# RWKV scan of a fused network on one core: the inverse of each chunk in seven products instead of ten, and the products with k and v on the other diagonal of the array

## The reference, cut to what matters

```
def _wkv_step(S, inp):
    r_t, w_t, k_t, v_t, a_t, b_t = inp
    sa = jnp.einsum('zbhvk,zbhk->zbhv', S, a_t)
    S = S * w_t[..., None, :] + sa[..., :, None] * b_t[..., None, :] + v_t[..., :, None] * k_t[..., None, :]
    return S, jnp.einsum('zbhvk,zbhk->zbhv', S, r_t)
```

## Time and profile before

| | |
|---|---|
| median of 3 runs | 4038.56 us (4037.82 to 4040.61) |
| span of the profiled execution (its own time is given as this span alone) | 4039.7 us |
| TensorE, DVE, ScalarE, GpSimd busy in the span | 3727.0, 2360.8, 1204.0, 1321.7 us |
| scan, first to last mask of a head | 2814.2 to 3365.6 us |
| walk of the last head in `walk_finish` | from some 3398.5 to 3424 us |

### The profile page before, as it was taken

The page is one execution under the profiler, slowest core; times in us unless marked ns, Lnnn a source line. Parts: engine busy times, 40 slices in busy tenths (PEclk is TensorE's granted clock), DMA queues, the critical chain, the costliest instruction groups (busy, mean ns, idle before and its releaser), DMA issues. The chain is left out here.

```text
span 4039.7 us, 81581 instructions
## 1 busy us (share of the span) xinstructions
PE 3727.0 (92%) x32706; PEld 2683.2 (66%) x32706; DVE 2360.8 (58%) x3864; ACT 1204.0 (30%) x2668; POOL 1321.7 (33%) x1020
## 2 busy tenths in 40 slices
PE   8888999898999999899999997998999999899887
PEld 6667878657787898777344444874999998733333
DVE  4568882545985445565444445767888776623333
ACT  3352222344222322331111112224455454111112
POOL 4443444434445364573000000431555453000000
PEclk9999999999999999999999999999999999899999
DMA  4114542303554122345999995356333234589997
GB/s 128 56 53 170 184 157 93 104 1 105 178 187 146 66 96 75 99 138 228 404 420 420 420 420 212 134 177 201 88 89 91 78 93 147 199 366 422 421 421 316
DMA packets 231204, 787.80 MB, mean 195 GB/s; under 512 B 56008, under 2 KB 64024, under 8 KB 171136
## 3 DMA queue, kind: packets, MB, share of 16 engines
q1 hardware_dynamic: 225008, 764.12, 50.9%
q0 software_dynamic: 5328, 19.40, 1.2%
q10 hardware_dynamic: 576, 0.09, 0.0%
HBM read 736.15 MB, written 47.38 MB: 194 GB/s over the span
## 5 line engine op out<-in xcount | busy, mean ns | idle before, releaser
L2887 POOL DMA_INDIRECT moe0e_xg<-moe_h,moe_first_rows x20 | 18.9, 947 | 546.3 <-DVE moe_first_rows L3044 540.5
L3011 ACT ACT_TABLE_LOAD x32 | 41.1, 1283 | 519.2 <-PE moe1e_p_u L2957 262.4
L373 POOL TENSOR_TENSOR gmi_w_lo<-gmi_rows_w,gmi_w_hi 128x512 fp32r<-128x512 f32 x64 | 120.2, 1878 | 159.8 <-ACT gmi_w_hi L415 159.8
L3960 PE MATMUL scan_bank<-scan_T,scan_off 64*64 64x64 f32 x3840 | 159.4, 220 | 8.5 <-issue 5.7
L373 POOL TENSOR_TENSOR p_w_lo<-p_rows_w,p_w_hi 128x512 fp32r<-128x512 f32 (+3 forms) x88 | 113.5, 1291 | 159.9 <-ACT p_w_hi L415 159.9
L2887 POOL DMA_INDIRECT moe1e_xg<-moe_h,moe_first_rows x17 | 16.0, 940 | 451.0 <-DVE moe_first_rows L3044 444.4
L1159 POOL TENSOR_TENSOR f0u_w_lo<-f0u_w,f0u_w_hi 128x1024 fp32r<-128x1024 f32 x42 | 115.0, 2757 | 137.6 <-ACT f0u_w_hi L1175 137.6
L1159 POOL TENSOR_TENSOR f1u_w_lo<-f1u_w,f1u_w_hi 128x1024 fp32r<-128x1024 f32 x42 | 114.3, 2742 | 137.5 <-ACT f1u_w_hi L1175 137.5
L1227 DVE SCALAR_TENSOR_TENSOR f0u_ada<-hT,condition,f0u_ada 128x512 f32<-128x512 f32 x168 | 148.2, 949 | 16.4 <-DMA hT<-in_ada_w_dram 15.9
L1227 DVE SCALAR_TENSOR_TENSOR f1u_ada<-hT,condition,f1u_ada 128x512 f32<-128x512 f32 x168 | 140.5, 903 | 20.5 <-DMA hT<-in_ada_w_dram 20.0
L2984 PE MATMUL moe0e_p_y<-moe_ring,moe0e_gatedT 128*64 128x512 f32 x608 | 137.6, 605 | 7.8 <-ACT moe0e_gatedT L3013 7.8
(11 more groups left out here) (903 smaller groups left out, 11529.7 us busy)
## 6 DMA issues: line engine op xcount, KB each, us to landing
moe_ring<-in_moe_w_down_dram SPq DMA_DIRECT2D x140, 1024.0 KB, 18.0
gm_uT<-in_moe_w_gu_dram SPq DMA_DIRECT2D x111, 1024.0 KB, 16.6
moe_ring<-in_moe_w_gu_dram SPq DMA_DIRECT2D x102, 1024.0 KB, 24.7
walk_memory<-in_moe_w_gu_dram SPq DMA_DIRECT2D x60, 1024.0 KB, 24.4
hT<-in_ada_w_dram SPq DMA_DIRECT2D x48, 1024.0 KB, 6.8
f0u_w<-in_ffn_w_gate_up_dram SPq DMA_DIRECT2D x22, 1024.0 KB, 4.8
f1u_w<-in_ffn_w_gate_up_dram SPq DMA_DIRECT2D x22, 1024.0 KB, 4.8
gmi_rows_w<-in_ga_w_in_dram SPq DMA_DIRECT2D x64, 256.0 KB, 2.7
```

Source lines behind the costliest of these rows:

```text
L373: nc.gpsimd.tensor_tensor(w_lo[t % 2][:, 0:width], w[t % RAW][:, 0:width], w_hi[t % 2][:, 0:width], ALU.subtract).then_inc(w_lo_made, 1)
L2887: pool.indirect_dma_start(xg[:], None, H.h, bass.IndirectOffsetOnAxis(rows[:, 0:1], 0)).then_inc(gathered, 16)
L3011: nc.scalar.activation(sg[:], p_g[:], ACT.Silu).then_inc(silu_ready, 1)
L3960: mm = nc.tensor.matmul(out[r], lhsT[r], rhs[r], start=start, stop=stop, skip_group_check=True)
```

## The change

The inverse is made by powers. A is split in three: joins of size 1 (first join), all joins of sizes 2 to 16 together (off), and the join of size 32 (off_outer). N = T times off is nilpotent; R is multiplied up by 1 + N, 1 + N^2, 1 + N^4 and 1 + N^8 while N is squared. There are seven products for each group of four chunks (n = 0 to 20): FIRST (off times T), three that square and multiply at once with 128 columns ([W | R] streamed through Z), LAST_POWER, OUTER (off_outer times T) and FINAL. The three wide ones are issued in two halves, so that 30 units (`UNITS`) keep the places of walk parts and factor slots. Each power is copied by ScalarE after DVE's addition (same bank) and transposed by DVE.

Direction 0's v now lies on hi and direction 1's on lo, and every product with kh or with v goes by `crossed`: hi rows to lo outputs and lo rows to hi outputs. Bonus rows and masks follow. Products with b and with k go to different banks and are issued in turn. Since a straight and a crossed product may not accumulate in one place at once, TensorE waits for its own products by four new semaphores. `walk_share` issues dS before the rows (in `walk_finish` it was after them), and x and y from v for the next chunk behind it. `walk_finish` has the same new walk (its diff repeats the one of the scan and is left out).

```diff
-LEVELS = 5
+BLOCK_BITS = 5
+PRODUCTS = 7
...
+    NI = PRODUCTS * NG
+    ADDED, COPIED, TURNED = 5 * NG, 5 * NG, 6 * NG
+    FIRST, LAST_POWER, OUTER, FINAL = 0, 4, 5, 6
+    UNITS = [(n, part) for n in range(NI) for part in ((0, 4),) * (n // NG not in (1, 2, 3)) + ((0, 2), (2, 4)) * (n // NG in (1, 2, 3))]
+    TURNS_BEFORE = (2, 3, 2, 3)
+    INV_BANK = (2, 1, 3, 0)
...
+    BPAIR_BANK, KPAIR_BANK = (4, 0, 2), (1, 3, 4)
+    TURN_BANKS = (slice(0, 2), slice(2, 4), slice(0, 2))
+    SLOTS = len(UNITS) // 2
...
-            for z, rows in ((0, lo), (1, hi)):
+            for z, rows in ((0, hi), (1, lo)):
...
+            if h:
+                pool.wait_ge(s["r_added"], h * ADDED)
             for g in range(NG):
+                g4 = slice(4 * g, 4 * g + 4)
                 pool.wait_ge(s["scaled"], h * NG + g + 1)
-                if h >= 2:
-                    pool.wait_ge(s["sa_ready"], (h - 1) * STEPS)
-                nc.gpsimd.tensor_tensor(R[u][:, 4 * g:4 * g + 4, :], strict(u, g), over4(join[:, 0, :]), ALU.mult).then_inc(s["r_joined"], 1)
-            for n in range(NZ):
-                l, g = n // NG, n % NG
-                if h:
-                    pool.wait_ge(s["z_ready"], (h - 1) * NZ + n + 1)
-                nc.gpsimd.tensor_tensor(off[n][:], strict(u, g), over4(join[:, l + 1, :]), ALU.mult).then_inc(s["off_ready"], 1)
+                nc.gpsimd.tensor_tensor(WR[:, g4, 1, :], strict(u, g), over4(join[:, 0, :]), ALU.mult).then_inc(s["r_joined"], 1)
+                nc.gpsimd.tensor_tensor(off[:, g4, :], strict(u, g), over4(join[:, 1, :]), ALU.mult).then_inc(s["off_ready"], 1)
+            for g in range(NG):
+                nc.gpsimd.tensor_tensor(off_outer[:, 4 * g:4 * g + 4, :], strict(u, g), over4(join[:, 2, :]), ALU.mult).then_inc(s["outer_ready"], 1)
...
             def copy_z(n):
-                act.wait_ge(s["z_ready"], h * NZ + n + 1)
-                if n >= 2:
-                    act.wait_ge(s["zr_ready"], h * NZ + n - 1)
-                A(Z[n % 2][:], quad(z_bank[n % 2]), ACT.Copy).then_inc(s["z_copied"], 1)
-            copy_z(0)
-            walk_part(walk, -1)
-            for n in range(NZ):
-                if n + 1 < NZ:
-                    copy_z(n + 1)
-                walk_part(walk, 2 * n)
-                walk_part(walk, 2 * n + 1)
-                if ahead is not None:
-                    factor_part(ahead, n)
+                act.wait_ge(s["inv_ready"], h * NI + n + 1)
+                A(Z[:, chunks(n), :], one(n), ACT.Copy).then_inc(s["z_copied"], 1)
+            def copy_power(n):
+                act.wait_ge(s["r_added"], h * ADDED + adds_through(n))
+                A(WR[:, chunks(n), 0, :], both(n)[:, :, 0, :], ACT.Copy).then_inc(s["z_copied"], 1)
+            for k, (n, (first, end)) in enumerate(UNITS):
+                if n // NG in (FIRST, OUTER):
+                    copy_z(n)
+                walk_part(walk, k - 1)
+                if squares(n) and end == 4:
+                    copy_power(n)
+                if ahead is not None and k % 2 == 0 and k:
+                    factor_part(ahead, k // 2 - 1)
+            walk_part(walk, len(UNITS) - 1)
...
+            def add_product(n):
+                g4 = chunks(n)
+                if n // NG == FIRST or n // NG == OUTER:
+                    return
+                dve.wait_ge(s["inv_ready"], h * NI + n + 1)
+                if squares(n):
+                    V.tensor_tensor(WR[:, g4, 1, :], WR[:, g4, 1, :], both(n)[:, :, 1, :], ALU.add).then_inc(s["r_added"], 1)
+                elif n // NG == LAST_POWER:
+                    V.tensor_tensor(WR[:, g4, 1, :], WR[:, g4, 1, :], one(n), ALU.add).then_inc(s["r_added"], 1)
+                else:
+                    if h >= 2 and n % NG == 0:
+                        dve.wait_ge(s["sa_ready"], (h - 1) * STEPS)
+                    V.tensor_tensor(R[u][:, g4, :], WR[:, g4, 1, :], one(n), ALU.add).then_inc(s["r_added"], 1)
+            def turn_product(n):
+                g4 = chunks(n)
+                if n // NG == FIRST:
+                    dve.wait_ge(s["z_copied"], h * COPIED + copies_through(n))
+                    turn(WR[:, g4, 0, :], Z[:, g4, :])
+                elif squares(n):
+                    dve.wait_ge(s["z_copied"], h * COPIED + copies_through(n))
+                    turn(Z[:, g4, :], WR[:, g4, 0, :])
+                elif n // NG == LAST_POWER:
+                    dve.wait_ge(s["r_added"], h * ADDED + adds_through(n))
+                    turn(T[:, g4, :], WR[:, g4, 1, :])
...
+            mask_b(0)
             scale(0)
-            mask(1)
-            mask(2)
+            mask_k(0)
+            mask_b(1)
             scale(1)
-            mask(3)
-            mask(4)
+            add_eye(0)
+            mask_b(2)
             scale(2)
-            add_eye(0)
+            mask_k(1)
             add_eye(1)
+            mask_k(2)
...
+                    add_product(n)
+                    if n:
+                        turn_product(n - 1)
...
+        def crossed(out, lhsT, rhs, start=True, stop=True):
+            for r, o in ((hi, lo), (lo, hi)):
+                mm = nc.tensor.matmul(out[o], lhsT[r], rhs[r], start=start, stop=stop, skip_group_check=True)
             return mm
+        def values_to_rows(i, lhsT, rhs, start=False):
+            for r, n in ((hi, i), (lo, lat - 1 - i)):
+                mm = nc.tensor.matmul(y_psum[side(n), n // 2 * HK:n // 2 * HK + HK], lhsT[r], rhs[r], start=start, stop=False, skip_group_check=True)
+            return mm
+        def values_to_x(w, j):
+            u = w % 2
+            return crossed(x_psum, pairs[u][:, j, 2, :], vs[u][:, j, :], stop=j == 0)
...
         def walk_state(w, j):
             u = w % 2
             if j == 0:
                 pe.wait_ge(v_loaded[u], (w // 2) * 32 + 32)
-            if j == 0:
-                mmul(x_psum, pairs[u][:, j, 2, :], vs[u][:, j, :]).then_inc(s["x_ready"], 1)
+                values_to_x(w, j).then_inc(s["x_ready"], 1)
                 if w:
                     pe.wait_ge(s["sm_ready"], w * (STEPS - 1))
-                mmul(ds_psum, bkT[u][:, j, 1, :], vs[u][:, j, :], stop=False)
             else:
-                mmul(x_psum, pairs[u][:, j, 2, :], vs[u][:, j, :], stop=False)
+                pe.wait_ge(s["xv_done"], w * (STEPS - 1) + j)
                 pe.wait_ge(s["sm_ready"], w * (STEPS - 1) + j)
                 mmul(x_psum, at(w, j), Sm[:], start=False).then_inc(s["x_ready"], 1)
-            if 0 < j < STEPS - 1:
-                mmul(ds_psum, bkT[u][:, j, 1, :], vs[u][:, j, :], stop=False)
-                mmul(ds_psum, eed[w % 3][:, j, :], Sm[:], start=False, stop=False)
+            if j < STEPS - 1:
+                crossed(ds_psum, bkT[u][:, j, 1, :], vs[u][:, j, :], stop=False).then_inc(s["dsv_done"], 1)
         def walk_solve(w, j):
-            u = w % 2
+            i = j - CSTEPS
             if j == 0:
-                pe.wait_ge(s["zr_added"], w * NZ + NZ)
+                pe.wait_ge(s["r_added"], w * ADDED + ADDED)
+            if i >= 0:
+                pe.wait_ge(s["yv_done"], w * lat + i + 1)
             pe.wait_ge(s["x_copied"], w * STEPS + j + 1)
             mmul(sa_psum, R[w % 2][:, j, :], X[:]).then_inc(s["sa_ready"], 1)
-            if j >= CSTEPS:
-                i = j - CSTEPS
-                if i == 0 and w:
-                    pe.wait_ge(s["y_copied"], w)
-                to_rows(i, rt(w, j), Sm[:], start=i == 0)
-                to_rows(i, pairs[u][:, j, 3, :], vs[u][:, j, :])
+            if j < STEPS - 1:
+                pe.wait_ge(s["dsv_done"], w * (STEPS - 1) + j + 1)
+            if 0 < j < STEPS - 1:
+                mmul(ds_psum, eed[w % 3][:, j, :], Sm[:], start=False, stop=False)
+            if i >= 0:
+                to_rows(i, rt(w, j), Sm[:]).then_inc(s["yr_done"], 1)
         def walk_share(w, j):
             u = w % 2
+            i = j - CSTEPS
+            if i >= 0:
+                pe.wait_ge(s["yr_done"], w * lat + i + 1)
             pe.wait_ge(s["sa_copied"], w * STEPS + j + 1)
             if j < STEPS - 1:
                 mmul(ds_psum, bkT[u][:, j, 0, :], SA[:], start=False).then_inc(s["ds_ready"], 1)
-            if j >= CSTEPS:
-                mm = to_rows(j - CSTEPS, pairs[u][:, j, 1, :], SA[:], stop=j - CSTEPS >= NT)
+            if i >= 0:
+                mm = to_rows(i, pairs[u][:, j, 1, :], SA[:], stop=i >= NT)
                 if j == STEPS - 1:
                     mm.then_inc(s["y_ready"], 1)
+            if j < STEPS - 1:
+                values_to_x(w, j + 1).then_inc(s["xv_done"], 1)
+                if i >= -1:
+                    if i == -1 and w:
+                        pe.wait_ge(s["y_copied"], w)
+                    values_to_rows(i + 1, pairs[u][:, j + 1, 3, :], vs[u][:, j + 1, :], start=i == -1).then_inc(s["yv_done"], 1)
...
+                    mm_b = mmul(bank[BPAIR_BANK[g]][:, o], bh[:, j, :], rhs)
```

(27 more changed lines are left out.)

285 lines of the change are left out of this document (144 added, 141 removed).

## The result

| | before | after |
|---|---|---|
| median | 4039.59 us (4 runs, 4037.82 to 4050.65) | 4068.31 us (4 runs, 4061.97 to 4077.66) |
| after / before | | 1.0065, 95% interval 1.0049 to 1.0081 |
| span of the profiled execution | 4039.7 us | 4075.8 us |
| first mask of the last head less that of the first, by 15 | 36.76 us | 39.29 us |

The account below looks back on a forecast made before the run. TensorE was taken as the bound, DVE close behind. Part A to +11.5 us plus part B of 22.2 gave 33.7 us a head instead of 36.76; with the last head and walk, 50 us less: 3989 us, range 3955 to 4018.

Parts of the forecast that it names:

- Waits added: TensorE's waits for its own crossed products in the walk: cost nothing; up to 0.43 us each if the cover were gone.
- The clock: TensorE's clock in the scan: 1.00 expected from 286 records in 10 us; a 1.2 GHz stretch only some 2 us.
- Crossed products cost nothing: On TensorE, a crossed product beside a straight one costs about nothing: pairs and turns 3.5 us instead of 7.0.
- The inverse: TensorE's array time for the inverse in each head: 14.1 us before, 13.4 after, only 0.7 us less.
- rival 3: No overlap: crossed products cost their full time and the 3.05 us a head are gone, 4037 us; chance 0.04.
- Part A: Pairs, turns and first walk steps of a head: DVE's shift ends at +11.0 us, wide products begin at +11.5.
- GpSimd's relief: GpSimd's 18 products become nine, free some 9 us into the head; DVE gains 0 to 1.9 us, taken as 1.2.
- Part B: Inverse units alternating with walk parts, from the wide products to the next head: 22.2 us in sum.
- bounds given for relief, collisions and idle time: Relief 0 to 1.9, collisions 0 to 2, idle 0.5 to 1.5 us: a head 32.2 to 35.5 us, 3967 to 4010.
- Number 2: TensorE runs short of instructions: 1.2 to 1.8 us a head return, about 4014 us; chance 0.13.
- Number 4: Slower: seven inverse stages in a row are too many; at 4.4 us a stage, 4058 us; chance 0.08.
- The last walk: dS issued before the rows from step 4 on: some 0.15 us in each of 7 steps, 1 us gained.

Follow-up runs that it names:

- e11: Changed kernel with TensorE's waits for its own row products (yv, yr) moved one product on, so each product in solve and share has one wait: 4047.63 us, 0.9999.
- e10: New inverse with straight products and the new walk order (4048.33 us), plus the four waits for own products, which nothing there needs: 4081.36 us, 1.0091.
- e12: e11 with the wait for x from v moved from TensorE to ScalarE's copy of the state: 4047.45 us, 1.0003.
- e13: e12 with ScalarE copying each power ahead of DVE's addition in the wide stages: 4044.16 us, 0.9999 of the kernel before.
- e6: Changed kernel with all b products first, then all k products, in each pair group and turn, still crossed: 4063.06 us, 1.0060.
- e8: e1 with ScalarE copying each power ahead of DVE's addition in the wide stages: 4046.18 us, 1.0006 of the kernel before.
- e18: e13 with 2 added products of 128 rows and 192 columns a head before turn 0: 4030.61 us, 0.9963 of the kernel before.
- e1: Changed kernel's inverse, pair groups and banks, but all products straight, the earlier walk and no waits for own products: 4045.87 us, 1.0008.

## Why the prediction was wrong, point by point

**The step that failed: "Waits added ... I cost them at nothing."** I priced them by latency (is the awaited product done in time?) and it was. The price is another: a second wait ahead of one product becomes an instruction, and it stands at the link through ScalarE, which I had reckoned at 0.65 us. 0.092 us more on some 25 links a head: 27 us by e11, 30 by e10. That is the whole 26 by which the kernel lost, and a third of the 76 between forecast and result. (By e12 the price holds in solve and share, not in state.) Of the other 50 some 20 are the clock by e13 (11 heads of 1.8 us), and 30 are the good head, 35.7 us against 33.7, in 15 heads.

**The clock, "I expect 1.00".** I divided records by time over a head, 286 in 10 us. The loss is local: it lies behind the stall at turn 0, and the head's mean does not show it. The forecast even names a stretch at 1.2 GHz "of some 2 us" without a price. It was 6.8 us, and 1.8 us a head in e13.

**Crossed products cost nothing: right on the array, half right on the time.** Records interleave as forecast; the rule that the prediction weighed against it (the Trainium skill, "TensorE: Matmul & The Clock Gate", Part 3: a weight load overlaps only with another row group) doesn't hold here: by the starts from 3119.42 on, bh and kh records of one half's rows and different outputs pass at twice the rate of straight ones. e6 shows that in the pairs this is worth nothing to the time. In all, crossing with its new order of the walk is worth 37.3 less 35.7, 1.6 us a head, where nothing spoils it (e8 and e18 at clock 1.00), against 3.0 in the forecast.

**The inverse: right.** I had given it 0.7 us of array time and, in rival 3, the whole change without overlap 4037 us, no gain. The inverse alone is 1.0008.

**Part A.** DVE's sum was right (+11.0; measured +11.2), GpSimd's relief too: 11.9 us of work, bonus 1.35 for 1.79, shift 0.42 for 0.94. "TensorE can have its three first products done by then" was wrong in the changed kernel (wide products at +14.1) and right without the stall and the second waits. In the first head of e18 shown above:

```profile
2955.33 0.22 PE L4008 MATMUL scan_bank<-scan_at_rt,scan_bh 64*64 64x64 f32 x1
...
2967.12 0.61 PE L4008 MATMUL scan_bank<-scan_WR,scan_Z 64*64 64x128 f32 x8
...
2991.01 0.22 PE L4008 MATMUL scan_bank<-scan_at_rt,scan_bh 64*64 64x64 f32 x1
```

The wide products start at +11.8 (forecast +11.5). **Part B** then takes 23.9 us where I had 22.2; the changed kernel needs 26.3 (3132.44 to 3158.76). The 1.7 us left were not followed up; a good head is 35.7, not 33.7.

**The range.** By the bounds given for relief, collisions and idle time, all at their worst or best, a head comes to 31.5 to 36.4 us and not 32.2 to 35.5; and 35.5 us a head would be some 4016, not 4010. The measured time lies above either.

**The rivals.** Number 2 saw the right mark, idle time without a releaser that doubles (15.3 to 30.2 us), but read it as a shortage of instructions, gave it 1.2 to 1.8 us a head and no effect on the clock; half of it went with the second waits (14.9 us in e11). Number 4, the one that ended slower, had the wrong mechanism: with the clock at 1.00 and no second waits, seven stages in a row are no loss (e1, e8). **The last walk** was to gain 1 us. Its y is copied here, against 3438.3 before:

```profile
L4603 ACT ACTIVATE rw_y_bonus<-rwf_bank x1: 384/384/384, 3477.9 to 3477.9; 128x256 f32<-128x256 f32 x1
```

From the last head's first mask that is 77.4 us instead of 72.7, of which the head itself has 2.6 (36.2 instead of 33.7, to the end of the scan). The walk lost about 2; its steps still wait twice in state and in share, but no run changed that.

## What to carry to other kernels

Count the waits ahead of each instruction on a chain through two engines: a second one can cost time even when it was satisfied long ago, at some links and not at others, so try each. Move it to the next product, or let the engine between them wait in its place. When TensorE's work shrinks but the chain around it stays, look at the granted clock in windows behind each stall, not over the whole loop, and compare heads of one run with and without a slow stretch: that gives its price at once. If it is worth it, try a few wide products in the stall, and as few as hold the clock: two did better here than seven. Many small ones were tried only in the changed kernel, with far more work, where seven wide ones gave no gain either.
